# RMS norms of row tiles: the inverse length goes to the rows on VectorE and ScalarE, and TensorE only transposes them

## What is computed

```python
def rmsnorm(x, gain):
    xf = x.astype(jnp.float32)
    y = xf * lax.rsqrt(jnp.mean(xf * xf, axis=-1, keepdims=True) + EPS)
    return (y * gain.astype(jnp.float32)).astype(x.dtype)
...
    for l in range(DEPTH):
        h = rmsnorm(x, g_mix[l])
        dq, dk, dv, c_q, c_kv_kr, xq, gate_logits = jnp.split(h @ w_in[l], split_idx, axis=-1)
...
        x = x + merged @ w_out[l]
        u = rmsnorm(x, g_mlp[l]) @ w_mlp1[l]
        x = x + jnp.square(jax.nn.relu(u)) @ w_mlp2[l]
```

## Time and profile before

| | us |
|---|---|
| median of 3 runs | 3684.78 (3683.88 to 3688.66) |
| profiled execution, its own time | 3687.42 |
| its span | 3686.1 |
| TensorE busy | 3500.5 (95%) |
| VectorE busy | 2082.2 (56%) |
| ScalarE busy | 1384.8 (38%) |
| L810 | 384 instructions of 0.270 to 0.552 us each |
| L849, 24 instructions | 6.7 |

### The profile page before, as it was taken

One profiled execution on the slowest core, in us unless ns is written; L12 is line 12 of the kernel. 1 busy time (PEld: TensorE's weight loads), 2 busy tenths in 40 slices (PEclk: granted clock), 3 DMA queues, 4 the chain that ended last, 5 costly groups with the idle time before them and its releaser, 6 DMA issues.

```text
span 3686.1 us, 56326 instructions
## 1 busy us (share of the span) xinstructions
PE 3500.5 (95%) x23512; PEld 2909.0 (79%) x23512; DVE 2082.2 (56%) x3862; ACT 1384.8 (38%) x2494; POOL 66.1 (2%) x32
## 2 busy tenths in 40 slices
PE   7999899999999899999999998998999989889999
PEld 7777688888888677788888887776888778778887
DVE  6777643544457676635444457754655578564434
ACT  5456543232234555433332233233332246232322
POOL 0000000000000000000000000000000033000000
PEclk9999999999999999999999989998999999889999
DMA  4221223233333221233333332234100323333332
GB/s 132 80 65 47 58 75 114 79 99 97 97 118 92 75 59 52 69 98 92 92 97 96 99 88 75 81 89 141 29 29 20 115 69 119 99 115 92 97 98 86
DMA packets 353827, 315.37 MB, mean 86 GB/s; under 512 B 11348, under 2 KB 281812, under 8 KB 353576
## 3 DMA queue, kind: packets, MB, share of 16 engines
q1 hardware_dynamic: 352712, 309.56, 28.0%
q10 hardware_dynamic: 864, 2.23, 0.2%
HBM read 288.15 MB, written 23.59 MB: 85 GB/s over the span
## 4 chain that ended last, share of the span: by engine, by line
PE 77%; DVE 14%; ACT 5%; issue 2%; DMA 1%; POOL 0%; DVEq 0%; ACTq 0%; SPq 0%; POOLq 0%
PE banks L508 12%; PE banks L510 12%; PE banks L509 12%; PE banks L411 8%; PE banks L413 8%; PE banks L412 8%; PE banks L2575 6%; DVE weights_r L352 2%; PE banks L2997 1%; PE banks L608 1%; ACT weights_high_r L345 1%; PE banks L1091 1%; PE banks L1078 1%; ACT probabilities L1227 1%; PE banks L810 1%
## 5 line engine op out<-in xcount | busy, mean ns | idle before, releaser
L352 DVE TENSOR_TENSOR weights_r<-weights,weights_high_r 128x1024 fp32r<-128x1024 f32 (+3 forms) x520 | 601.7, 1164 | 499.0 <-ACT weights_high_r L345 498.1
L508 PE MATMUL banks<-h_T_hi,weights_high_r 128*128 128x512 f32 (+2 forms) x1904 | 762.2, 400 | 30.4 <-DVE h_T_lo L855 17.4
L510 PE MATMUL banks<-h_T_hi,weights_r 128*128 128x512 f32 (+2 forms) x1904 | 740.2, 389 | 0.0
L509 PE MATMUL banks<-h_T_lo,weights_high_r 128*128 128x512 f32 (+2 forms) x1904 | 740.1, 389 | 0.0
L345 ACT ACTIVATE weights_high_r<-weights 128x1024 fp32r<-128x1024 f32 (+3 forms) x520 | 510.5, 992 | 396.5 <-DMA weights<-in_w_mlp 220.3
L508 PEld LDWEIGHTS banks<-h_T_hi,weights_high_r 128*128 128x128 f32 x1904 | 364.4, 191 | 116.6 <-issue 41.0
L510 PEld LDWEIGHTS banks<-h_T_hi,weights_r 128*128 128x128 f32 x1904 | 363.8, 191 | 72.1
L509 PEld LDWEIGHTS banks<-h_T_lo,weights_high_r 128*128 128x128 f32 x1904 | 364.6, 191 | 69.2 <-issue 3.4
L411 PE MATMUL banks<-weights_high_r,h_T_hi 128*128 128x512 f32 (+3 forms) x704 | 290.3, 412 | 13.3 <-DVE h_T_lo L855 5.6
L413 PE MATMUL banks<-weights_high_r,h_T_lo 128*128 128x512 f32 (+3 forms) x704 | 265.8, 378 | 0.0
L412 PE MATMUL banks<-weights_r,h_T_hi 128*128 128x512 f32 (+3 forms) x704 | 265.7, 377 | 0.0
(11 more groups left out here) (545 smaller groups left out, 5729.2 us busy)
## 6 DMA issues: line engine op xcount, KB each, us to landing
weights<-in_w_in SPq DMA_DIRECT2D x182, 512.0 KB, 3.8
weights<-in_w_mlp SPq DMA_DIRECT2D x128, 512.0 KB, 3.8
weights<-in_ffn_w_in SPq DMA_DIRECT2D x44, 512.0 KB, 3.8
weights<-in_w_out SPq DMA_DIRECT2D x24, 512.0 KB, 3.6
weights<-in_ffn_w_down SPq DMA_DIRECT2D x22, 512.0 KB, 3.3
weights<-in_w_mem_kv SPq DMA_DIRECT2D x16, 512.0 KB, 3.6
weights<-in_w_diff_o SPq DMA_DIRECT2D x16, 512.0 KB, 3.7
weights<-in_w_mla_o SPq DMA_DIRECT2D x8, 512.0 KB, 3.4
```

The costliest lines, as they stand in the source:

```text
L352: ve.e.tensor_tensor(self.part(c.w_raw_r, u), self.part(c.w_raw, u), self.part(c.w_high_r, u).bitcast(F32), ALU.subtract).then_inc(*ve.tel ...
L508: pe.e.matmul(out, lhsT=wh[:, k, :], rhs=hi[k][:, cols], start=(k == 0), stop=False)
L509: pe.e.matmul(out, lhsT=wh[:, k, :], rhs=lo[k][:, cols], start=False, stop=False)
L510: mm = pe.e.matmul(out, lhsT=wl[:, k, :], rhs=hi[k][:, cols], start=False, stop=(k == self.chunks - 1))
```

## The change

The diagonal matrices go. After the root, VectorE multiplies the first half of the row in `xg` by the inverse length, in place (128x512). At its step `turn, t` ScalarE does the same to the second half, ahead of its two copies from the banks. TensorE then transposes the blocks with its transpose operation against the identity; it waits for VectorE's half before bank 0 and for ScalarE's half before bank 1. The cell that held the diagonals is no longer used.

```diff
     def pe(self):
         c, pe = self.c, self.c.pe
         for kind, t in self.order:
             if kind == "turn":
-                pe.wait_ge("gained", self.tag, t, 1)
-                pe.wait_ge("diagonal", self.tag, t)
                 for g in range(2):
+                    pe.wait_ge("scaled", self.tag, t, g)
                     bank = c.fill(self.tag, t, g, ring=self.ring)
                     for k in range(4):
                         at = (4 * g + k) * P
-                        mm = pe.e.matmul(bank[:, k * P:(k + 1) * P], lhsT=self.xg[:, t, at:at + P], rhs=self.diagonals[:, t * P:(t + 1) * P],
-                                         start=True, stop=True)
+                        mm = pe.e.transpose(bank[:, k * P:(k + 1) * P], self.xg[:, t, at:at + P], c.ident[:, :])
                     mm.then_inc(*pe.tell("filled", self.tag, t, g))
...
     def act(self):
...
             else:
+                xg = self.halves(self.xg[:, t, :])[1]
+                ac.wait_ge("gained", self.tag, t, 1)
+                ac.wait_ge("inverse_root", self.roots[t - t % self.together].tag)
+                ac.e.activation(xg, xg, ACT.Copy, scale=self.sums[0][:, t:t + 1]).then_inc(*ac.tell("scaled", self.tag, t, 1))
                 for g in range(2):
                     ac.wait_ge("filled", self.tag, t, g)
...
     def dve(self):
...
                     for j in some:
-                        ve.e.tensor_scalar(self.diagonals[:, j * P:(j + 1) * P], c.ident[:, :], self.sums[0][:, j:j + 1], None,
-                                           ALU.mult).then_inc(*ve.tell("diagonal", self.tag, j))
+                        xg = self.halves(self.xg[:, j, :])[0]
+                        ve.wait_ge("gained", self.tag, j, 0)
+                        ve.e.tensor_scalar(xg, xg, self.sums[0][:, j:j + 1], None, ALU.mult).then_inc(*ve.tell("scaled", self.tag, j, 0))
```

More of the change, by code:

```diff
@@ L772, with __init__ @@
     n = len(ORDER)
-    def __init__(self, c, tag, x_ready, gain, gain_in, dumps, diagonals, xg, free, cells_free, store=None, ring="work", pairs=False):
+    def __init__(self, c, tag, x_ready, gain, gain_in, dumps, xg, free, cells_free, store=None, ring="work", pairs=False):
         self.order, self.together = (self.IN_PAIRS, 2) if pairs else (self.ORDER, 1)
         self.c, self.tag, self.x_ready, self.gain, self.gain_in = c, tag, x_ready, gain, gain_in
-        self.dumps, self.diagonals, self.xg, self.free, self.cells_free, self.store, self.ring = dumps, diagonals, xg, free, cells_free, store, ring
+        self.dumps, self.xg, self.free, self.cells_free, self.store, self.ring = dumps, xg, free, cells_free, store, ring
         self.sums = [c.tile_sums[:, h * NT:(h + 1) * NT] for h in range(2)]
@@ L1586, in wide_norm_cells @@
     first = c.places["S"][0]
-    return c.wide_cells(first, 2), [c.cell(first + 2), c.cell(first + 4)], c.cell(first + 3)
+    return c.wide_cells(first, 2), [c.cell(first + 2), c.cell(first + 4)]
 class Layer1:
```

## The result

The changed kernel takes 3698.92 us (median of 5 runs, 3695.25 to 3704.43), the kernel before 3684.78 beside it (5 runs): a ratio of 1.0039, with a 95% interval of 1.0024 to 1.0053, slower by 14.1 us. Predicted were 3703 us, 18.4 above before. The profiled execution took 3695.57 us, 8.15 more than that of before; it is one of the two fastest of the five.

The account below looks back on a forecast made before the run. TensorE, busy 95% of the span, was taken as the bound. Terms 7.1 + 5.4 + 1.0 + 2.1 - 4.6 + 3.9 + 3.5 = 18.4 us on the 3684.78 us median gave 3703 us, range 3691 to 3718.

Parts of the forecast that it names:

- Transposes: TensorE's turns: eight transposes replace eight true products, saving 0.91 us a turn where nothing waits; -4.6 us over five norms.
- ScalarE's scaling: New 128x512 ACTIVATE in front of a waiting TensorE: taken as 0.72 us, bounds 0.63 and 0.73.
- tile 2: Third turn in four MLP norms: only VectorE's longer instruction counts in the chain TensorE already waits for; +1.0 us.
- Tile 1: Second turn in the five norms beside products: TensorE waits for ScalarE's half, +1.07 us each, 5.4 in all.
- tile 2 at 1078: Third turn in the norm at 1078 us, without the usual wait behind it: ScalarE arrives late, +2.1 us.
- Tile 0: First turn in the five norms beside products: +1.5 us in four and 1.1 in one, 7.1 us in all.
- The first norm: Kernel's first norm, working in pairs: scaling, turns by halves and copies in series delay it by 3.9 us, bounds 2 and 5.
- The clock: TensorE's granted clock: new waits cause two falls, 3.5 us, within bounds of 0 and 19 us.
- Those falls stay: Clock falls already present after long waits, as in the first MLP norm, remain; no term in the sum.
- Scaled in time, the transposes pay: Rival: ScalarE reaches the turn when TensorE does, so the turns gain; about 3666 us, faster; chance 0.06.
- The waits are swallowed: Rival: TensorE's existing waits for L855 absorb the first two turns' delay in three norms; 3690 us; chance 0.14.
- The clock falls in most turns: Rival: each of 11 waiting turns loses 1.7 to 3 us to half clock; 3724 us; chance 0.12.

Follow-up runs that it names:

- the first experiment: Changed kernel, but in the five norms beside products ScalarE scales its half earlier, behind the square of the next tile's first half; 3671.84 us, 0.9970 of the kernel before.

## Why the prediction was right

**The mechanism** was right at each step. ScalarE comes to the turn 1.55 us behind TensorE, scales for 0.71 us, and the turn is longer instead of shorter; moved in the order, the same instruction makes TensorE wait in no tile 0, 1 or 2. The forecast of 3703 is 4 us above the median, by sizes of terms and by one term that it left out, under the clock below:

- *Transposes.* 0.91 us saved in tile 3, as predicted, five times. The runs differ from the factor of four for FP32 that the Trainium skill gives ("TensorE: Matmul & The Clock Gate", section Terms): eight blocks in one piece took 1.03 us with the last one's 0.27 in it, 0.109 from one to the next, against 0.223 for a true product.
- *ScalarE's scaling*: 0.72 taken, 0.706 measured. *VectorE's*: 0.546 taken from a row on another tile, 0.486 measured, so +0.20 and not +0.26 us a tile. This is more than half of what tile 2 came out lower (0.6 for 1.0).
- *Tile 1*: 5.1 for 5.4, *tile 2 at 1078*: 2.3 for 2.1, with 0.35 us of it from half the clock.
- *Tile 0*: 6.4 for 7.1. I had read the row at 696 as the pattern of four norms. Where VectorE's chain, which a weight load starts, ends behind TensorE's last product, TensorE waits ahead of the turn, and this wait differs from trace to trace. In the last block's first norm TensorE had waited 0.55 us for L849 before its turn; in the change that wait is gone, so the turn grew by only 0.57. In layer 1's MLP norm it grew by 2.11, most of the excess by a new wait ahead of the turn, here in the change:

```profile
1751.89 0.66 PE L809 MATMUL banks<-identity,cellsA 128*128 128x128 f32 x4 [0.58 <-DVE cellsA L853]
1754.46 0.93 PE L809 MATMUL banks<-identity,cellsA 128*128 128x128 f32 x4 [1.91 <-ACT cellsA L828]
```

The clock adds 0.17 us inside this turn. The second trace of the change has 0.33 us in place of the 0.58, and the run with only the first norm changed has 0.20 in place of the 0.55, so single values of this row hold some tenths of a microsecond that are not the change's.
- *The first norm*: 3.9 predicted, 2.8 at the restart, and 2.2 (-1.5 to 4.8, from the interval of the ratio) in the run with it alone. The term that was mis-sized is the end of the first pair: its last subtraction on VectorE ended at 21.58, 0.5 later than 21.10, where I had 1.2, since ScalarE was at the first scaling at 15.94 and not at 16.35, and the pair's turns ended at 20.2, where I had 20.7. VectorE's scaling added 0.4, as predicted. So ScalarE's second pair began at 36.34, 0.9 later than 35.47 instead of 1.6, and from there to the restart it took 1.9 us more, where I had 2.3.

```profile
37.10 1.97 PE L809 MATMUL banks<-identity,cellsA 128*128 128x128 f32 x8 [7.40 <-ACT cellsA L828]
39.51 1.12 PE L809 MATMUL banks<-identity,cellsA 128*128 128x128 f32 x4 [0.44 <-ACT cellsA L828]
40.27 0.67 PE L411 MATMUL banks<-weights_high_r,h_T_hi 128*128 128x384 f32 x1
```

- *The clock*: 3.5 us taken for two falls. The trace has two new ones, those at 1086.06 and 1754.46 (a second trace of the change has a third, at tile 0 of the first MLP norm). They cost 3.0 us, 0.5 inside the turns and 2.5 behind them, and filling the waits gained 4.1. What the prediction put at nothing are the falls that stay (*Those falls stay*). They start in the waits around tile 2's second half, ahead of the restart, and the restart now comes later in them: in the first MLP norm the half clock ran from 718.03 and TensorE restarted at 718.78, in the change it runs from 720.46 and TensorE restarts at 723.34, both for 6.8 us. In three norms this gives back 0.8 to 1.0 us, 2.8 in all, and in the second trace 2.4.

Turns and falls come to 12.7 + 2.5 - 2.8 = 12.4 us, and the two profiled executions are 8.15 apart. Of the difference 2.7 us lie between 2153 and 3296 us, where the run with only the first norm changed, with its five norms as before, has the same (2.8 less than before): it is the profiled execution of before that was longer there. The other 1.5 us lie between norms too and are not explained; in the second trace these places go both ways. The profiled execution of before was 2.6 us above its median and that of the change 3.4 below, so that 8.15 and the medians' 14.1 are the same difference. By its two traces the spread of the changed kernel's runs does not come from the turns in the main: these, of 3695.57 and 3701.14 us, have 173.0 and 193.5 us at half the clock in all, and only 3.4 of the 20.5 us between them are a fall at a turn. What moves the others was not tried.

That the forecast is as near as 4 us is luck in part: the turns without the clock were put 2.7 us too high (14.9 for 12.2), and the 2.8 us given back at the restarts were not in it. Its chances have a slip that changes nothing: slower than before adds up to 0.87, not 0.86.

**The rivals.** *Scaled in time, the transposes pay* would have been right with another order, which the first experiment made: 11.8 us faster, not 21.9. In its trace tiles 0 and 1 have the full gain of some 0.9 us each. Tile 2 gains nothing in the four norms with a wait behind it (-0.04 to +0.20 us), tile 3 of layer 1's first norm waits 1.13 us for ScalarE, which scales it behind an L345, and the first norm restarts 3.1 us later. *The waits are swallowed* fell: behind tile 2 the whole delay of tiles 0 and 1 arrives at the restart (TensorE was 4.29 us late ahead of that turn and 4.56 behind it in the first MLP norm), so the restart is 2.5 us later against the norm's first turn, which was 2.04 late (2.8 predicted). *The clock falls in most turns* fell for the change, where two or three of eleven did; with the wait at 2.3 us instead of 1.7 it came nearer (new falls at eight of the eleven turns in the trace). The rule behind it, in the Trainium skill, "TensorE: Matmul & The Clock Gate", section PE-mode transpose, that transposes do not count as busy in the same way, is not borne out by the kernel before, in another stage. There TensorE has nothing but 32 transposes for 9.8 us, in groups of four with waits of 0.2 to 1.65 us, and the granted clock stays at 1.00 and falls only at 3144.91, when products run again:

```profile
3134.12 0.60 PE L608 MATMUL banks<-identity,cellsX 128*128 128x128 f32 x4
...
3143.94 0.47 PE L508 MATMUL banks<-h_T_hi,weights_high_r 128*128 128x512 f32 x1 [1.65 <-DVE h_T_lo L636]
```

```profile
3137.50:3140.90 3.40, 1.79 (x13) 1.08 (x11) 2.33 (x4) 2.27 (x4) 0.00 (x0) 1.00 0.90 304
3140.90:3144.30 3.40, 1.54 (x10) 1.05 (x11) 2.49 (x4) 2.65 (x4) 0.00 (x0) 1.00 0.29 88
```

Each of the seven plain waits of more than 5 us in that trace, leaving out the one at the start, had the clock at 0.50 before it ended. So transposes do hold the clock here; whether as well as products do is not shown.

## What to carry to other kernels

A cheaper instruction on the bounding engine gains only if its operands are there when its turn comes; ask of each new producer not what share of the span its engine is busy, but which instruction stands ahead of it and who releases that one. Here the producer stood behind a square that waited for TensorE's own last product, a loop of 1.55 us, while earlier, in a gap of up to 5 us, the engine was idle and for part of it the operand ready. Place such an instruction where its inputs are complete, not where its result is consumed.

## What was not expected of the hardware

A wait of TensorE that is a little longer can cost more than its length. From 1.71 to 2.32 us of waiting in tile 1's turn, the growth was 0.61 us of wait and, at the turns where the granted clock then went to 0.5 (1.2 GHz), products 0.43 us apart in place of 0.23; 18 us in all where the waits alone were to make 9. The falls went from two or three of eleven turns to eight. In the change's own waits, work that nobody reads kept the clock at 1.00 through all eleven turns of its trace.
